# Constants, filter network, filter spectra and first norm of a diffusion backbone step: four stages or one

## What is computed

```python
def _rmsnorm(x, g):
    y = x * lax.rsqrt(jnp.mean(x * x, axis=-1, keepdims=True) + EPS)
    return y * g

def _hyena_filters(L, w1, b1, w2, b2, w3, freq):      # for L = 1024 and for L = 256
    ...
    h = jnp.sin(fr * (emb @ w1 + b1))
    h = jnp.sin(fr * (h @ w2 + b2))
    h = (h @ w3).reshape(L, 2, HYENA_ORDER, D_HYENA)   # 2 directions, 2 orders, 512 channels
    h = h * jnp.exp(-t * jnp.abs(deltas))[:, None, None, :]
    fwd, bwd = h[:, 0], h[:, 1]
    two_sided = jnp.concatenate([fwd[:1] + bwd[:1], fwd[1:], zeros, bwd[1:][::-1]], axis=0)
    return jnp.fft.rfft(two_sided, axis=0)

def _layer(x, mod, ...):
    shift1, scale1, gate1, shift2, scale2, gate2 = jnp.split(mod, 6, axis=-1)  # mod = silu(c) @ w_ada + b_ada
    h = _rmsnorm(x, norm1_g) * (1.0 + scale1) + shift1
    proj = h @ w_in
    ...
```

## Time and profile before

| | |
|---|---|
| median of 3 runs | 3179.49 us (3178.71 to 3181.02) |
| the profiled execution: its own time | 3175.44 us |
| its span | 3173.7 us |
| PE busy over the span | 2787.0 us (88%) |
| from the start to the first transfer of `stage_heads` | 382.37 us |
| PE busy in that part | 236.6 us |

### The profile page before, as it was taken

One profiled execution on the slowest core, in us unless ns is written; L12 is line 12 of the kernel. 1 busy time (PEld: TensorE's weight loads), 2 busy tenths in 40 slices (PEclk: granted clock), 3 DMA queues, 4 the chain that ended last, 5 costly groups with the idle time before them and its releaser, 6 DMA issues. The chain is left out here.

```text
span 3173.7 us, 36289 instructions
## 1 busy us (share of the span) xinstructions
PE 2787.0 (88%) x14926; PEld 2342.5 (74%) x14926; DVE 1372.1 (43%) x1846; ACT 862.0 (27%) x1384; POOL 848.5 (27%) x590
## 2 busy tenths in 40 slices
PE   4887199888999999999878837979899999999998
PEld 3765188776877888787766735868788888888886
DVE  4552689932555544444367653122622122122115
ACT  1110311111545544444331133111412211211221
POOL 1452368831100110010023302212223322322330
PEclk9978599999999999999989977989999999999999
DMA  3357267744212232121185655351011011111101
GB/s 109 119 173 225 92 211 237 232 152 154 71 64 94 87 110 76 64 89 39 57 290 197 225 199 205 131 201 53 27 40 40 34 41 40 35 40 40 40 27 67
DMA packets 106237, 351.41 MB, mean 111 GB/s; under 512 B 12792, under 2 KB 27641, under 8 KB 105754
## 3 DMA queue, kind: packets, MB, share of 16 engines
q1 hardware_dynamic: 78218, 241.61, 21.7%
q0 software_dynamic: 27856, 107.49, 10.1%
HBM read 254.16 MB, written 86.51 MB: 107 GB/s over the span
## 5 line engine op out<-in xcount | busy, mean ns | idle before, releaser
L292 PE MATMUL tl_b<-tl_hi,tl_whi 128*128 128x512 f32 (+1 forms) x960 | 344.7, 359 | 20.1 <-DVE tl_lo L2204 14.6
L293 PE MATMUL tl_b<-tl_lo,tl_whi 128*128 128x512 f32 (+1 forms) x960 | 342.5, 357 | 0.0
L294 PE MATMUL tl_b<-tl_hi,tl_wlo 128*128 128x512 f32 (+1 forms) x960 | 341.7, 356 | 0.0
L2145 DVE SCALAR_TENSOR_TENSOR tl_x<-tl_b,all_mod,tl_x 128x512 f32<-128x512 f32 (+1 forms) x216 | 142.6, 661 | 374.3 <-PE tl_b L294 363.3
L2039 POOL TENSOR_TENSOR tl_wlo<-tl_raw,tl_whi 128x1024 fp32r<-128x1024 f32 x72 | 178.3, 2478 | 444.6 <-ACT tl_whi L1958 444.6
L292 PE MATMUL at_out<-h_hi,at_whi 128*128 128x512 f32 (+1 forms) x672 | 266.7, 397 | 13.1 <-POOL at_wlo L688 10.5
L292 PE MATMUL tl_b<-tl_uhi,tl_whi 128*128 128x512 f32 (+1 forms) x768 | 274.9, 358 | 3.5 <-POOL tl_ulo L2049 3.5
L294 PE MATMUL tl_b<-tl_uhi,tl_wlo 128*128 128x512 f32 (+1 forms) x768 | 276.7, 360 | 0.0
L293 PE MATMUL tl_b<-tl_ulo,tl_whi 128*128 128x512 f32 (+1 forms) x768 | 274.6, 357 | 0.0
L864 DVE TENSOR_REDUCE at_nmax<-at_s 128x1 f32<-128x1280 f32 (+1 forms) x160 | 196.8, 1272 | 146.0 <-PE at_s L740 146.0
L688 POOL TENSOR_TENSOR at_wlo<-at_raw,at_whi 128x1024 fp32r<-128x1024 f32 x28 | 66.0, 2357 | 670.6 <-ACT at_whi L788 670.6
(11 more groups left out here) (274 smaller groups left out, 6122.7 us busy)
## 6 DMA issues: line engine op xcount, KB each, us to landing
tl_raw<-in_w_tail SPq DMA_DIRECT2D x72, 512.0 KB, 3.3
hy_tab<-in_hy_tab POOLq DMA_DIRECT2D x68, 512.0 KB, 5.2
flt_tab<-in_filt_tab POOLq DMA_DIRECT2D x44, 512.0 KB, 5.4
hd_wa<-in_w_adaT SPq DMA_DIRECT2D x32, 512.0 KB, 3.7
at_raw<-in_w_proj SPq DMA_DIRECT2D x28, 512.0 KB, 4.6
s_spec<-flt_ob POOLq DMA_DIRECT2D x44, 256.0 KB, 5.1
s_gatesT<-at_pad SPq DMA_DIRECT2D x16, 640.0 KB, 2.9
mg_gate<-s_gatesT SPq DMA_DIRECT2D x16, 640.0 KB, 5.1
```

Of the source, the lines that this page charges most:

```text
L292: pe.matmul(out, w_hi, x_hi, start=first, stop=False)
L293: pe.matmul(out, w_hi, x_lo, start=False, stop=False)
L294: return pe.matmul(out, w_lo, x_hi, start=False, stop=last)
L2145: dve.scalar_tensor_tensor(out=x1[:, n, at:at + m], in0=bank[x % GEMM_BANKS][:, 0:m], scalar=g.mod[:, gate, SEG_OF[c]:SEG_OF[c] + 1], in1= ...
```

## The change

The four stages become one, `stage_head` (tiles `fd_`). What it does, part by part:

- **Network.** The weights w1, w2 and the vectors are doubled by the host, so that a matmul gives 128 rows, the second 64 equal to the first. The layers go chunk by chunk (512, 512, 256 columns), each chunk with its own semaphores; the six DVE steps are made per chunk. The first five modulation units stand on PE between the chunks of the second layer.
- **Taps.** w3 is doubled too; DVE adds its directions on rows 0 to 63 and subtracts them on rows 64 to 127 (L1251, L1252). So the taps come out of PE as sums and differences. A pair still has 12 matmuls, but six on rows 0 to 63 and six on rows 64 to 127, side by side in different banks (L1029). ACT's copies and DVE's L1307 and L1308 are gone; DVE multiplies by the decay out of PSUM (L1198).
- **Modulation.** All 16 units stand in the beginning and in the first order: 5, then 3, 2, 2, 2, 2 behind the five pairs. The weights go through three slots.
- **Spectra.** The context units come first in each order; tables are loaded at the size that is used, and their first loads are issued behind the first pair's low parts. ACT, not DVE, scales the units (L1110).
- **Norm.** The three slots then carry the eight x tiles for the squares (ACT, L1103, and DVE, L1221, between the units of the first order) and again for the result. Sums, root and diagonals stand between the two orders, the spreading matmuls (three) behind the last pair. DVE multiplies (L1228), ACT adds the shift and rounds (L1118), DVE forms the low part (L1236), between the units of the second order.

```diff
-    return lat + [(0, 2)] + ctx + [(LAT_FT, 2)]
+    return ctx + [(LAT_FT, 2)] + lat + [(0, 2)]
...
+STREAM = 3
+ADA_FIRST, ADA_BY_PAIR = 5, [3, 2, 2, 2, 2, 0, 0, 0, 0, 0]
+EARLY = {8: 0, 15: 1}
...
+    ITEMS = [("ada", n) for n in range(FIRST_ADA)] + [("x", k) for k in range(KD)] + [("h", k) for k in range(KD)]
...
+            def load(i):
+                if i >= STREAM:
+                    kind, n = ITEMS[i - STREAM]
+                    sp.wait_ge({"ada": ada_mm, "x": summed, "h": h_l}[kind], n + 1)
...
-                for i in range(4):
-                    tile = 2 * p + i // 2
-                    mm = products(pe, bank[i][:], h_hi[:, tile * P:(tile + 1) * P], h_lo[:, tile * P:(tile + 1) * P],
-                                  w3_hi[:, i % 2, o], w3_lo[:, i % 2, o], True, True)
-                mm.then_inc(taps, 1)
+                for i in range(2):
+                    tile = slice((2 * p + i) * P, (2 * p + i + 1) * P)
+                    for f, w, start, stop in ((f_hi, w3_hi, True, False), (f_hi, w3_lo, False, False),
+                                              (f_lo, w3_hi, False, True)):
+                        for d in range(2):
+                            rows = slice(HID * d, HID * d + HID)
+                            mm = pe.matmul(tap_bank[2 * i + d][:], f[rows, tile], w[rows, o], start=start, stop=stop)
...
+            for i in range(NET):
+                layer(0, i)
+            modulation(1)
+            for i in range(NET):
+                layer(1, i)
+                modulation(1)
+            modulation(ADA_FIRST - 1 - NET)
...
+                if o:
+                    pe.wait_ge(diag_done, 1)
+                    pe.wait_ge(mixed, 2 * PAIRS)
+                    for c, (at, m) in enumerate(CHUNKS):
+                        mm = pe.matmul(spread_bank[c][:, 0:m], g.ones[:], diag[:, at // P:(at + m) // P, :], start=True,
+                                       stop=True)
...
+                if o == 0:
+                    pe.wait_ge(summed, KD)
+                    pe.wait_ge(scaled, M)
+                    for tt in range(TT):
+                        mm = pe.matmul(p_sum[:, tt:tt + 1], acc[:, tt * P:(tt + 1) * P], g.ones[:, 0:1], start=True,
+                                       stop=True)
...
+            for p in range(PAIRS):
+                split(0, p)
+            for u in range(M):
+                scale(u)
+                if u % 2 and u // 2 < KD:
+                    square(u // 2)
+            act.wait_ge(var_done, 1)
+            act.activation(std[:], var[:], ACT.Sqrt).then_inc(std_done, 1)
+            for p in range(PAIRS):
+                split(1, p)
...
+            for u in range(M):
+                scale(M + u)
+                k, odd = divmod(u - FILT_CTX_U, 2)
+                if odd == 0 and 0 <= k < KD:
+                    shift(k)
```

680 lines of the change are left out of this document (315 added, 365 removed).

## The result

The changed kernel takes 3043.63 us (median of 4 runs, 3041.68 to 3048.53) where the kernel before takes 3179.55: 0.9574 of the time, with a 95% interval from 0.9559 to 0.9589. A second measurement gave 3043.02 against 3178.86. They save 135.9 and 135.8 us. The forecast was 3055.1 with a range from 3040 to 3074: the direction was right, the size 11.5 us short.

The account below looks back on a forecast made before the run. It took four barrier-separated stages (382.4 us, PE busy 236.6) to lose every wait; merged, the next stage starts at 258.0, 124.4 us less, so 3175.4 becomes 3051.0, plus 4.1 to the median, 3055.1 us; range 3040 to 3074.

Parts of the forecast that it names:

- Network: Start of the kernel: PE through the network at 33.2 us, five modulation units (17.5) included, where it was 45.7.
- First pairs: Pairs of the first order: six matmul times per pair, PE through at 84.4 us, spectra starting at 85.7.
- Taps serial: Rival in the pairs: tap matmuls do not run two at once, 18 us more, 3073; chance 0.05.
- First spectra: First order's spectra: 57.5 us plus 5 for x transfers (bounds 0 and 11.5), 62.5 in all, ending at 148.2.
- Transfers bind: Rival in the spectra: no lead left, x transfers count in full, 15 us more, 3070; chance 0.13.
- Transfers fit: Rival: x loads lie in the tables' lead, diagonals do not alternate, 3046, or 3040 with the clock; chance 0.22.
- Scaling on ACT: First spectra: with ACT scaling, the DVE waits (3.3 us and one like it) and cold matmuls behind them go.
- Middle: Between the orders: 41 us, diagonals until +17.6, POOL's low parts ending at +40.8; 38 or 44.8 as alternatives.
- Second spectra: Second order's spectra: 56.5 us plus 1 for five x tiles (bounds 0 and 9.6), ending at 246.7.
- The norm is not covered: Rival: DVE's and ACT's norm steps run out behind the last unit, 9 us more, 3064; chance 0.06.
- The rule that the prediction held against the change: Spectra: DVE steps on SBUF operands could delay each POOL table issue by some 1.5 us.
- 30 slots, 6 less: First pairs: if PE's clock rises, 30 tap slots of 0.43 us become 0.23, 6 us less, 3040.

Follow-up runs that it names:

- mod_behind: Changed kernel with the network's five modulation units behind its second layer, not between its chunks; 3051.83 us.
- taps_serial: Changed kernel with each pair's six tap matmuls on rows 0 to 63 listed first, then the six on rows 64 to 127; 3053.27 us.
- x_fifth: Changed kernel loading only the last 256 of 1280 columns of each x tile for the squares; 3043.22 us.
- store_first: Changed kernel with POOL issuing a unit's store before the load of a later table, not behind it; 3048.48 us.
- scale_dve: Changed kernel with DVE, not ACT, scaling the units, as in the kernel before; 3049.32 us.
- diag_act: Changed kernel with the ten diagonal tiles made by ACT behind the splits of pairs 0 and 1, not by DVE; 3043.94 us.
- diag_act_split: Changed kernel with the diagonals on ACT and the second order's pairs 0 and 1 split before the root; 3041.45 us.
- norm_behind: Changed kernel with x tiles for the norm's result loaded only after the last unit of the second spectra; 3066.02 us.
- split_first: Changed kernel with ACT splitting pairs 0 and 1 of the second order before the root, diagonals still on DVE; 3044.29 us.

## Why the prediction was right, and where it was off

**Network: right.** 33.2 against 32.8, the lambda matmul at 4.54 and not 5.5. That five units would fill PE's waits is what mod_behind shows: 11.3 us.

**First pairs: right in the sum, wrong in one detail.** Six slots of 0.43 per pair hold (9.77 from pair to pair). PE was to be through at 84.4; it was at 82.1 in the first profile, because the last two units ran at the higher clock (3.89 us at 78.18). The additions on DVE were to be slow beside POOL, some 8 us a pair. They are not, since POOL is idle by the time they run: four take 2.4. It was covered by PE either way. *Taps serial* falls: even where the list has them six by six, taps_serial is only 1.02 us a pair longer, not 2.56.

**First spectra: 60.45 for 62.5; two terms mis-sized against each other.** The transfers cost 0.7 to 2.3 us and not 5 (x_fifth), because 363 GB/s, which I took for the ceiling, was no ceiling: the same trace has 403 from 50 to 60 us. The demand was mis-sized too, the other way: by the prediction's own terms the first 17 units last 43.9 us (57.5 less five of 2.72) and not 45.6, which makes 424 GB/s and not 408. Against this the start at the lower clock had twelve slow starts and not six, 1.2 us more, and at each early pair four starts stand 0.32 to 0.34 apart instead of 0.23, which adds 0.35 to the 0.5 allowed. That gives 59.1, and x_fifth measured 59.2. *Transfers bind* falls. *Transfers fit* was nearest in time and on the transfers, with a load of 404 to 417 GB/s and no reserve (store_first), but its other half, diagonals that do not alternate, is wrong: they took 10.26 us.

**Scaling on ACT: right in kind.** The wait of 3.31 at an early pair is gone; scale_dve brings 2.2 and eight matmuls at the lower clock back.

**Middle: 38.3 for 41, its head mis-sized.** The token sums took 2.8 us at a granted clock of 0.83, where the norm of before took 4.4 at 0.50, so the diagonals began at +4.4 and not at +6.4; they took 10.3 and not 11. The rest of the chain was as foretold: the prediction had the multiplications of the last three pairs at +17.6, +22.9 and +30.3, that is 5.3 and 7.4 us apart, and measured are +14.6, +20.2 and +27.6, 5.6 and 7.4 apart (DVE's L1198 at 161.76, 167.35 and 174.78). So it had DVE's 7.4 us a pair right. The expectations of diag_act and diag_act_split dropped that term and went wrong by it.

**Second spectra: 55.8 for 57.5.** No stall at all: x came late, but DVE's steps behind it had time. *The norm is not covered* falls by norm_behind: 21 us by position and 26 by the medians come back when its second half is uncovered. The rule that the prediction held against the change did not show either: POOL's 44 table issues took 0.53 to 0.89 us, with DVE's steps on SBUF operands beside them.

**The sum: inside the range, and outside the 3050 to 3060 that the forecast gave itself.** 5.4 us of the 11.5 are these steps. The other 6 are that the medians save 135.9 and 135.8 where the profiled parts save 129.7 and, second profile against second, 126.1. The prediction had carried a saving of one profiled execution over to the median as it was. The profiled executions of before lie 4.1 and 2.4 us below their medians, those of the changed kernel 4.9 and 2.5 above theirs. A part of it is the clock of the first pairs, a rival that the prediction had weighed at "30 slots, 6 less" and that comes in some executions. Nine of the kernels here have the same instructions up to the first spectra (x_fifth loads less of x near their end). In them S1 was 86.73 to 87.00 five times and 79.67, 82.60, 82.61 and 84.50 four times, on the average 1.9 us before the first profile's 86.75. The rows of diag_act's pairs, and PE's granted clock in the two stretches:

```profile
63.09 0.63 PE L1029 MATMUL fd_tap<-fd_w3lo,fd_fhi 64*128 64x512 f32 x2
...
65.36 3.87 PE L1014 MATMUL fd_mod<-all_silu,fd_in 128*128 128x2 f32 x32
...
69.16 0.80 PE L1029 MATMUL fd_tap<-fd_w3hi,fd_fhi 64*128 64x512 f32 x2
```

```profile
62.50:65.20 2.70, 2.70 (x13) 1.83 (x12) 1.36 (x3) 1.25 (x3) 0.54 (x1) 0.50 0.74 203
65.40:69.00 3.60, 3.60 (x34) 3.60 (x32) 3.39 (x6) 0.74 (x2) 3.60 (x4) 0.97 0.39 107
```

Two modulation units take 3.87 us at the granted clock of 0.97, the higher level, and the taps around them run at 0.50, the lower. Each pair with the higher clock is 3.1 us shorter, and that comes from the modulation, not from the taps as the rival had it. Three pairs of this execution have it, and S1 is 4.1 us earlier, since PE then waits longer for POOL (6.71 us). In both profiles of before no unit in the pairs had the higher clock. The other 4 us or so stay open: they are within what single executions scatter. That the time still fell into the range owes something to its width.

## What to carry to other kernels

Stages that wait for one engine's chain in turn (PE for the sine, PE for POOL, DVE for PE) are worth more merged than sped up. The norm's own stage of 74 us is gone; what it costs now is a part of the middle and about 1 us of transfers in the first spectra, and of its cover only the second half was tested, at 21 to 26 us. 11 us are modulation units in a place where PE had to wait. When two pools of steps are to overlap, ask first for the buffers, not for the engines: diag_act freed DVE of 10 us and gained 2, because the next pair needed a buffer that POOL was reading. A transfer rate seen in a trace is what that kernel asked for, averaged over the stretch that was chosen; it bounds nothing from above unless something waits for it at that moment. When a position in a profile moves, look first whether it had moved already in front of the edit.

## What the runs showed of the hardware

- The DMA engines moved 404 to 417 GB/s over 35 us, in a mix of loads and stores; the kernel before had 403 over 10 us, in loads alone.
- Matmuls of depth 64 on the two halves of the rows run at once even when the list has them six by six: the second half's first started together with the third of the first half, and the twelve took 1.02 us more than side by side, where six slots of 0.43 would be 2.56.
- The clock changed within one pair: modulation units at the higher level between taps at the lower (diag_act), in some executions and not in others of the same program. Nine profiles with the same instructions up to the first spectra start them at 79.67 to 87.00 us.
- The ten one-operand diagonals took 2.05 us alone and 10.26 with nine POOL steps beside them, eight of them one POOL step each. In split_first they took 7.32, 5.56 of it a single one that waited until POOL had finished; four multiplications out of PSUM took 2.48 in every case.
- The record of the granted clock reads 1.00 from the start of an execution up to its first change, though matmuls of 512 columns start 0.43 us apart there.
